# Windowed attention of a fused four-layer kernel: pairs of heads kept together, weights divided by the row sums, values on column halves

## The reference

```
p = softmax(concatenate([s_sink, s_meta, s_band]))      # s_sink: one learned number for each head
o = p[..., 1:1+16] @ meta_v + p[..., 17:] @ vband        # float32 throughout
```

## Time and profile before

| | us |
|---|---|
| median of 3 timed runs | 4331.46 (4327.49 to 4334.54) |
| the profiled execution | 4335.81 |
| its span, from the first to the last instruction | 4334.0 |
| PE busy | 4029.7 (93%) |
| DVE busy | 1845.5 (43%) |
| ACT busy | 1441.6 (33%) |
| mean granted clock of PE | 0.952 of full speed |
| sweep of layer 0, 2457.4 to 2625.8 | 168.4 |
| sweep of layer 1, 3561.4 to 3707.6 | 146.2 |

### The profile page before, as it was taken

The page is one execution under the profiler, slowest core; times in us unless marked ns, Lnnn a source line. Parts: engine busy times, 40 slices in busy tenths (PEclk is TensorE's granted clock), DMA queues, the critical chain, the costliest instruction groups (busy, mean ns, idle before and its releaser), DMA issues.

```text
span 4334.0 us, 66723 instructions
## 1 busy us (share of the span) xinstructions
PE 4029.7 (93%) x28114; PEld 3570.8 (82%) x28114; DVE 1845.5 (43%) x3401; ACT 1441.6 (33%) x2876; POOL 466.6 (11%) x529
## 2 busy tenths in 40 slices
PE   6988899999989999899989989979997998997998
PEld 6866678888878777788878869979996886997998
DVE  3443454323334444544445444343335544434344
ACT  3444443212233333332322343333232224434322
POOL 1211120000012222100010000020002000002001
PEclk8988899999989999999999979989998998998999
DMA  4022112222331110133311102322321110222332
GB/s 165 25 88 83 52 39 72 98 98 98 98 107 44 35 34 28 40 103 101 103 53 40 49 18 69 91 63 89 93 83 44 40 45 23 77 91 65 93 93 74
DMA packets 86762, 303.75 MB, mean 70 GB/s; under 512 B 9392, under 2 KB 12592, under 8 KB 86336
## 3 DMA queue, kind: packets, MB, share of 16 engines
q1 hardware_dynamic: 84944, 292.72, 21.5%
q0 software_dynamic: 1520, 6.75, 0.5%
HBM read 297.34 MB, written 2.10 MB: 69 GB/s over the span
## 4 chain that ended last, share of the span: by engine, by line
PE 87%; ACT 5%; DVE 3%; POOL 2%; issue 2%; DMA 2%; ACTq 0%; SPq 0%; DVEq 0%; POOLq 0%
PE bank L472 58%; PE bank L534 6%; PE bank L954 3%; PE bank L825 2%; PE bank L503 2%; PE bank L803 2%; PE bank L943 2%; PE bank L740 1%; POOL scratch L2402 1%; PE bank L779 1%; PE bank L1046 1%; PE bank L624 1%; PE bank L813 1%; PE bank L1019 1%; PE bank L685 1%
## 5 line engine op out<-in xcount | busy, mean ns | idle before, releaser
L1688 DVE TENSOR_TENSOR weight_lo<-weight_raw,weight_hi 128x1024 fp32r<-128x1024 f32 (+1 forms) x464 | 561.5, 1214 | 564.3 <-ACT weight_hi L1123 564.1
L472 PE MATMUL bank<-u_hi,weight_hi 128*128 128x256 f32 (+1 forms) x2368 | 692.3, 292 | 8.0 <-DVE u_lo L2342 5.8
L472 PE MATMUL bank<-u_lo,weight_hi 128*128 128x256 f32 (+1 forms) x2368 | 678.4, 286 | 0.0
L472 PE MATMUL bank<-u_hi,weight_lo 128*128 128x256 f32 (+1 forms) x2368 | 677.6, 286 | 0.0
L1123 ACT ACTIVATE weight_hi<-weight_raw 128x1024 fp32r<-128x1024 f32 (+1 forms) x464 | 476.3, 1031 | 504.9 <-PE bank L472 370.6
L472 PE MATMUL bank<-h_hi,weight_hi 128*128 128x512 f32 (+1 forms) x1360 | 500.1, 368 | 24.2 <-DVE h_lo L2073 12.9
L472 PE MATMUL bank<-h_lo,weight_hi 128*128 128x512 f32 (+1 forms) x1360 | 478.4, 352 | 0.0
L472 PE MATMUL bank<-h_hi,weight_lo 128*128 128x512 f32 (+1 forms) x1360 | 478.0, 351 | 0.0
L472 PEld LDWEIGHTS bank<-u_hi,weight_hi 128*128 128x128 f32 x2368 | 454.8, 192 | 27.4 <-issue 17.6
L472 PEld LDWEIGHTS bank<-u_hi,weight_lo 128*128 128x128 f32 x2368 | 454.8, 192 | 0.0
L472 PEld LDWEIGHTS bank<-u_lo,weight_hi 128*128 128x128 f32 x2368 | 453.7, 192 | 0.1
(11 more groups left out here) (270 smaller groups left out, 7587.3 us busy)
## 6 DMA issues: line engine op xcount, KB each, us to landing
weight_raw<-in_w_mlp SPq DMA_DIRECT2D x128, 512.0 KB, 3.6
weight_raw<-in_w_ff SPq DMA_DIRECT2D x128, 512.0 KB, 3.6
weight_raw<-in_w_in SPq DMA_DIRECT2D x92, 512.0 KB, 3.6
weight_raw<-in_w_mod SPq DMA_DIRECT2D x80, 512.0 KB, 3.9
weight_raw<-in_a_w_qkv SPq DMA_DIRECT2D x24, 512.0 KB, 4.3
weight_raw<-in_b_w_qkv SPq DMA_DIRECT2D x24, 512.0 KB, 3.6
first_weight<-in_w_mod SPq DMA_DIRECT2D x16, 512.0 KB, 14.7
weight_raw<-in_w_ret_o SPq DMA_DIRECT2D x16, 512.0 KB, 3.6
```

Of the source, the lines that this page charges most:

```text
L472: m = e.matmul(view[:, 0:hi - lo], a[:, k, :], b[:, k0 + k, lo:hi], start=(k == 0 and i == 0), stop=(k == kt - 1 and i == 2))
L1688: e.tensor_tensor(wlo[s][:, 0:kt, :], raw[n % N_RAW][:, 0:kt, :], whi[s][:, 0:kt, :].bitcast(F32), ALU.subtract).then_inc(*tick("dve_split ...
```

## The change

A unit is now a pair of heads: 20 units in layer 0 and 16 in layer 1, with three calls of `fill` for each as before, so that each call hands out twice as much. Scores are computed as before. DVE masks both heads and then takes both maxima. ACT takes both exponentials in place. DVE then takes one reciprocal of two sums and multiplies the weights of each head by theirs, in place, in SBUF. PE turns both heads' weights, ACT copies them to `WWT`, of which there is one buffer for each head (before, `PT` had two that alternated over the units). For the values the operands trade places: the 64 columns of `AV` of a head are stationary and its turned weights (128 queries) stream. Head 0 uses columns 0 to 63 of the array and head 1 columns 64 to 127, matmul by matmul in turn, into the two halves of one bank. The output comes out with features on the partitions, so that `AON`, the turn of the output (L1057) and the scaling of it (L2307) are gone; ACT copies the bank to `OA` at the beginning of the next unit.

```diff
-        AON = sb("win_rows", [P, 5, P], F32, o_z + 6 * HYB + 2560)
...
-        S_ = [W_S[:, 416 * i:416 * i + 416] for i in range(2)]
-        P_ = [W_S[:, 832 + 416 * i:832 + 416 * i + 416] for i in range(2)]
-        PT = [W_S[:, 1664 + 512 * i:1664 + 512 * i + 512] for i in range(2)]
-        QUERY_PAD = W_S[:, 2688:2944].rearrange("p (s c) -> p s c", s=2)
+        WS = [[W_S[:, 416 * (2 * i + s):416 * (2 * i + s) + 416] for s in range(2)] for i in range(2)]
+        WWT = [W_S[:, 1664 + 512 * s:1664 + 512 * s + 512] for s in range(2)]
...
-        WINDOW = [[(pr, qi, sub) for pr in range(4) for qi in range(5 - layer) for sub in range(2)]
-                  for layer in range(2)]
+        WINDOW = [[(pr, qi) for pr in range(4) for qi in range(5 - layer)] for layer in range(2)]
...
-                    pr, qi, sub = units[i]
-                    if sub:
-                        return
+                    pr, qi = units[i]
...
-                    views = [take("s", 2, layer, i + s) for s in range(2)]
...
-                                m.then_inc(*tick(("pe_scoreu", "pe_scorel")[s], ("s", 2, layer, i + s)))
-                    close("s", 2, layer, i)
-                    close("s", 2, layer, i + 1)
+                                m.then_inc(*tick(("pe_scoreu", "pe_scorel")[s], ("s", 2, layer, i, s)))
+                    for s in range(2):
+                        close("s", 2, layer, i, s)
...
-                    view = take("t", 2, layer, i)
-                    e.wait_ge(*at("w", 2, layer, i))
-                    Pr = P_[i % 2][0:nq]
-                    for j in range(len(ts)):
-                        e.transpose(view[:, P * j:P * j + nq], Pr[:, 17 + P * j:17 + P * j + P], ident[0:nq, 0:nq])
-                    e.transpose(view[0:N_META, 384:384 + nq], Pr[:, 1:17], ident[0:nq, 0:nq]).then_inc(
-                        *tick("pe_turn", ("t", 2, layer, i)))
-                    close("t", 2, layer, i)
+                    for s in range(2):
+                        view, x = take("t", 2, layer, i, s), WS[i % 2][s][0:nq]
+                        e.wait_ge(*at("n", 2, layer, i, s))
+                        for j in range(len(ts)):
+                            e.transpose(view[:, P * j:P * j + nq], x[:, 17 + P * j:17 + P * j + P], ident[0:nq, 0:nq])
+                        e.transpose(view[0:N_META, 384:384 + nq], x[:, 1:17], ident[0:nq, 0:nq]).then_inc(
+                            *tick("pe_turn", ("t", 2, layer, i, s)))
+                        close("t", 2, layer, i, s)
...
-                    pr, qi, sub = units[i]
...
-                    T_, gs = PT[i % 2], slice(HD * sub, HD * sub + HD)
...
+                    _, nq, ts, _ = geometry(units[i][1])
                     view = take("o", 2, layer, i)
-                    e.wait_ge(*at("wt", 2, layer, i))
+                    e.wait_ge(*at("wt", 2, layer, i, 0))
+                    e.wait_ge(*at("wt", 2, layer, i, 1))
                     e.wait_ge(*at("wvd", layer))
-                    e.matmul(view[0:nq, 0:HD], T_[0:N_META, 384:384 + nq], AV[0:N_META, 4, gs], start=True, stop=False)
-                    for n_, j in enumerate(ts):
-                        m = e.matmul(view[0:nq, 0:HD], T_[:, P * n_:P * n_ + nq], AV[:, j, gs],
-                                     start=False, stop=(n_ == len(ts) - 1))
+                    keys = [(4, N_META, 384)] + [(j, P, P * n) for n, j in enumerate(ts)]
+                    for k, (j, nk, c) in enumerate(keys):
+                        for s in range(2):
+                            r = slice(HD * s, HD * s + HD)
+                            m = e.matmul(view[r, 0:nq], AV[0:nk, j, r], WWT[s][0:nk, c:c + nq], start=(k == 0),
+                                         stop=(k == len(ts)))
                     m.then_inc(*tick("pe_value", ("o", 2, layer, i)))
                     close("o", 2, layer, i)
...
-                def turn_out(i):
-                    pr, qi, sub = units[i]
-                    _, nq, _, _ = geometry(qi)
-                    if sub == 1:
-                        view = take("ot", 2, layer, i)
-                        e.wait_ge(*at("out", 2, layer, i))
-                        e.transpose(view[:, 0:nq], AON[0:nq, qi, :], ident[0:nq, 0:nq]).then_inc(
-                            *tick("pe_value", ("ot", 2, layer, i)))
-                        close("ot", 2, layer, i)
-
-                sweep(len(units), (score, nothing, turn_weights, values, nothing, turn_out), fill)
+                sweep(len(units), (score, nothing, turn_weights, values, nothing, nothing), fill)
...
-                    n = 17 + P * len(ts)
-                    e.wait_ge(*at("max", 2, layer, i))
-                    if i >= 2:
-                        e.wait_ge(*at("t", 2, layer, i - 2))
-                    e.activation(P_[i % 2][0:nq, 0:n], S_[i % 2][0:nq, 0:n], ACT.Exp, bias=w_small(i, 0, nq),
-                                 accum_out=w_small(i, 1, nq)).then_inc(*tick("act_attn", ("w", 2, layer, i)))
+                    for s in range(2):
+                        x = WS[i % 2][s][0:nq, 0:17 + P * len(ts)]
+                        e.wait_ge(*at("max", 2, layer, i, s))
+                        e.activation(x, x, ACT.Exp, bias=w_small(i, s, nq), accum_out=w_small(i, 2 + s, nq)).then_inc(
+                            *tick("act_attn", ("w", 2, layer, i, s)))
...
-                    view, T_ = view_of("t", 2, layer, i), PT[i % 2]
...
-                    e.wait_ge(*at("t", 2, layer, i))
-                    if i >= 2:
-                        e.wait_ge(*at("o", 2, layer, i - 2))
-                    e.activation(T_[:, 0:P * len(ts)].rearrange("p (j c) -> p j c", c=P)[:, :, 0:nq],
-                                 view[:, 0:P * len(ts)].rearrange("p (j c) -> p j c", c=P)[:, :, 0:nq], ACT.Copy)
-                    e.activation(T_[0:N_META, 384:384 + nq], view[0:N_META, 384:384 + nq], ACT.Copy).then_inc(
-                        *tick("act_attn", ("wt", 2, layer, i), ("free", "t", 2, layer, i)))
+                    if i:
+                        e.wait_ge(*at("o", 2, layer, i - 1))
+                    for s in range(2):
+                        view, to = view_of("t", 2, layer, i, s), WWT[s]
+                        e.wait_ge(*at("t", 2, layer, i, s))
+                        e.activation(to[:, 0:P * len(ts)].rearrange("p (j c) -> p j c", c=P)[:, :, 0:nq],
+                                     view[:, 0:P * len(ts)].rearrange("p (j c) -> p j c", c=P)[:, :, 0:nq], ACT.Copy)
+                        e.activation(to[0:N_META, 384:384 + nq], view[0:N_META, 384:384 + nq], ACT.Copy).then_inc(
+                            *tick("act_attn", ("wt", 2, layer, i, s), ("free", "t", 2, layer, i, s)))
 
...
-                    if sub == 1:
-                        e.wait_ge(*at("ot", 2, layer, i))
-                        e.activation(OA[:, pr, q0:q0 + nq], view_of("ot", 2, layer, i)[:, 0:nq], ACT.Copy).then_inc(
-                            *tick("act_attn", ("free", "ot", 2, layer, i), ("oa", layer, pr)))
-
-                sweep(len(units), (score, expo, turn_weights, nothing, nothing, turn_out), fill)
+                    e.wait_ge(*at("o", 2, layer, i))
+                    e.activation(OA[:, pr, q0:q0 + nq], view_of("o", 2, layer, i)[:, 0:nq], ACT.Copy).then_inc(
+                        *tick("act_attn", ("free", "o", 2, layer, i)))
+
+                sweep(len(units), (score, expo, turn_weights, nothing, turn_out, nothing), fill)
...
-                    job = ("s", 2, layer, i)
-                    view, S = view_of(*job), S_[i % 2][0:nq]
-                    e.wait_ge(*at(*job))
-                    if i > 1:
-                        e.wait_ge(*at("w", 2, layer, i - 2))
-                        e.wait_ge(*at("out", 2, layer, i - 2))
-                    e.tensor_scalar(S[:, 1:1 + N_META], view[0:nq, 0:N_META], SCALE, None, ALU.mult)
-                    e.scalar_tensor_tensor(out=S[:, 17:17 + nb], in0=view[0:nq, N_META:N_META + nb], scalar=SCALE,
-                                           in1=mask, op0=ALU.mult, op1=ALU.add).then_inc(
-                        *tick("dve_attn", ("sc", 2, layer, i), ("free", *job)))
-                    e.wait_ge(*at("sc", 2, layer, i))
-                    e.wait_ge(*at("sink", layer, i))
-                    e.tensor_reduce(w_small(i, 0, nq), S[:, 0:17 + nb], AX, ALU.max, negate=True).then_inc(
-                        *tick("dve_attn", ("max", 2, layer, i)))
-
-                def values(i):
-                    pr, qi, sub = units[i]
-                    _, nq, ts, _ = geometry(qi)
-                    e.wait_ge(*at("w", 2, layer, i))
-                    e.reciprocal(w_small(i, 2, nq), w_small(i, 1, nq)).then_inc(*tick("dve_attn", ("rc", 2, layer, i)))
+                    for s in range(2):
+                        job = ("s", 2, layer, i, s)
+                        view, x = view_of(*job), WS[i % 2][s][0:nq]
+                        e.wait_ge(*at(*job))
+                        if i > 1:
```

(41 more changed lines are left out.)

10 lines of the change are left out of this document (5 added, 5 removed).

## The result

| | before | after |
|---|---|---|
| time, median (lowest to highest), us | 4333.0 (4327.49 to 4337.46), 4 runs | 4238.38 (4231.45 to 4239.26), 4 runs |
| ratio after / before, 95% interval | | 0.9779 (0.9762 to 0.9796) |
| both sweeps, us | 314.6 | 210.1 |
| PE busy / idle in them, us | 276.5 / 38.1 | 196.5 / 13.5 |

The account below looks back on a forecast made before the run. The prediction took the sweeps to be bound by PE, with stalls. Its terms, -48.7 - 7 + 2 + 4 = -49.7, rounded to -49, gave 4282 us, with a range of 4248 to 4316.

Parts of the forecast that it names:

- Work of PE: In both sweeps, 234.5 us at full clock, to fall by 41.3: 34.1 from values, 7.2 from the output's turn.
- Halves in turn: Rival for the values: column halves run in turn, not at once; 4312 to 4316 us, chance 0.03.
- With the share of half clock unchanged, 41.3 x 276.5 / 234.5 = 48.7 us.: Step for PE in the sweeps: saved full-clock work, stretched by an unchanged half-clock share, gives 48.7 us.
- the 0.80 to 0.92: Sign for both sweeps: a clock outside this range would show the prediction wrong; about 0.85 was expected.
- clock recovers: Rival for the sweeps: shorter stalls let the clock stay full, up to 34 us more saved; 4248 us, chance 0.11.
- I expect the long stalls to stay: Argument against the clock recovering in the sweeps; a long stall at 2578.5 to 2581 was followed by half clock.
- Taken together 0: Term for PE's stalls before the turns, 14.0 us in the kernel before: no net change, from -8 to +15.
- + 2 + 4: Terms in the total: scores, turns and fill up to +2; each layer's first unit waiting about 1.9 longer, +4.
- The places rotate, so 16 x 0.87 = 14 us: Term for stalls before the turns: 16 sigmoids with table loads, at rotating places in the fill, cost 14 us.
- A weight split that falls on a reload adds about 2: Term for stalls before the turns: a weight split of 1.04 us meeting a table reload adds about 2.
- The longer chain: Rival: the loop turn, copies, exponentials, multiply, next turn binds; 33 us come back, 4315 us, chance 0.14.
- 36 times 0.3 is 11 us: Term for PE's wait for ACT's copies before the values: 11 us against 17.9, so -7, bounds -18 and +5.

Follow-up runs that it names:

- e2: Kernel after with the two loops of the values swapped, so all key tiles of one column half precede the other's; 4260.76 us.
- e10: Kernel after with two added ACT copies of 384 columns in every unit, behind the wait for the second head's turned weights; 4263.75 us.
- e12: Kernel after with four added ACT copies of 960 columns in every fourth unit, behind the wait for the second head's turned weights; 4292.57 us.
- e6: Kernel before with a plain copy in place of the gates' sigmoid in the sweeps, those gates missing from the result; 4290.9 us.
- e3: Kernel before with heads in pairs and nothing else of the change: values as before, outputs divided instead of weights; 4291.75 us.
- e11: Kernel after with each weight tile multiplied once more, into a place that nobody reads; 4241.71 us.
- e4: Kernel before with each value matmul streaming all 128 columns of AV instead of 64, the others left unused; 4330.1 us.
- e9: e1 with each value matmul streaming all 128 columns of AV instead of 64, the others left unread; 4294.49 us.
- e1: Kernel after with the values computed as before and the turn of the output they need; weights still divided; 4294.33 us.

## Why the prediction was wrong

The direction and the mechanism of the values held; the size did not, by half.

**Work of PE: right, a little high.** PE was busy for 89.8 us of before's half clock, a share of 0.94 where the working took 0.88. Taken to full clock its work was thus 231.7 us and not 234.5, and it fell to 194.8, by 37 against 41.3 forecast. A pair with three band tiles takes 1.17 us from its start to the next instruction, against 1.08. Halves in turn were priced at 1.9 us for such a pair and 34.1 - 9 = 25 us more for the values. e2 has 2.28 from start to next and 33 us more of work, about what the values cost before the change; its time is only 22 more, since less is idle. The Trainium skill, TensorEngine Tiling (Array Packing), Key Properties, has the change of mode drain TensorE. The row above agrees with a small cost: 8 pairs of instructions at 0.118 are 0.95, and the rest of 1.17 is 0.22 for the step from 16 rows to 128 and the way back to full width together. No run separates the two, and what the entry costs does not show in it.

**The step that failed: "With the share of half clock unchanged, 41.3 x 276.5 / 234.5 = 48.7 us."** It took half clock as a tax on work, so less work paid less of it. The tax (half of PE's busy time at half clock) fell from 45 us to 2, 43 us less where the step allowed 7. The clock left the 0.80 to 0.92 that the prediction had set as a sign of being wrong. e10 and e12 show what it mostly hangs on here: long gaps of PE. At nearly the same idle sum the one has 13.7 us at half clock and the other 71.7. And e6 shows that in the kernel before the long gaps came from the table loads: none of them, no long gap, and 75 us less at half clock. The rival "clock recovers" had this mechanism and its 34 us, with a chance of 0.11. What spoke against it, "I expect the long stalls to stay", was the second error.

**"Taken together 0": the stalls before the turns.** They fell from 14.0 us to 6.3. (The sum carried + 2 + 4 for them, not the 0 of their own paragraph, and so expected 20.) The term that failed is "The places rotate, so 16 x 0.87 = 14 us". The working charged a sigmoid 1.1 us ahead of the copies, 1.5 between the copies and the exponentials, and nothing in the last fill. By ACT in order of time, 14 sigmoids stand in the two sweeps of after, and 9 of them in the last fill. Two stand ahead of the copies (2532.82 and 2555.64; the values then wait 0.92 and 0.40 us). Three stand between (2541.48, 2564.07, 3565.64), and PE waits 0.82, 2.23 and 0.64 for the multiply. At the working's own prices that is 2 x 1.1 + 3 x 1.5 = 6.7 us, not 14. In before, six stood between copies and exponentials, and they have 12.3 of the 14.0 us and all five long stalls. So the costly place is held by half as many, each at a smaller price; what part each has in it no run separates. A sigmoid in the last fill:

```profile
2524.23 0.19 ACT L1552 ACTIVATION_READ_ACCUMULATOR scratch<-scratch,small 128x1 f32 x1
2524.43 1.28 ACT L1469 ACT_TABLE_LOAD   x1
2525.73 0.40 ACT L1469 ACTIVATE hybrid_tmp<-bank 128x272 f32<-128x272 f32 x1
...
2527.53 0.49 ACT L1562 ACTIVATE scratch<-bank 128x384 f32<-128x384 f32 x1 [1.24 <-PE bank L1027]
...
2528.71 1.28 ACT L1552 ACT_TABLE_LOAD   x1
2530.01 0.63 ACT L1552 ACTIVATE scratch<-scratch,small 128x401 f32<-128x401 f32 x1
```

The load for the sigmoid starts straight behind the exponentials; load, sigmoid and one output copy are done by 2526.3, and ACT is then idle for 1.24 us before PE's turns release the copies. That part costs the chain nothing, as the working had it. The load back starts with the last copy's end and does lie on the chain, 1.28, but against a cover of two heads' values, fill and scores, 3.75 us by the prediction's own sum. The rows of before show the same order: a load at 2589.45, and 2.39 us of idle behind its sigmoid. The Trainium skill, ScalarE: Activation LUTs, What ACT_TABLE_LOAD costs, gives 2.66 us for a change of set, a load of 1.28 and a drain of 1.38. These rows show the load's 1.28 and no drain: the next ACTIVATE starts 1.30 after the load does.

ACT's idle time behind PE's turns, in layer 0, before and after (us, times, longest):

```profile
ACT scratch L1576 <- PE bank L1033: 86.0, 37, 5.9
```

```profile
ACT scratch L1562 <- PE bank L1027: 32.2, 17, 3.5
```

With one head at a time ACT had 86 us of idle and yet was late for PE: it could only work ahead by one head. The pair doubles what can be done at a time. e3, which has the pairs alone, shows the fall of PE's idle time from 38.1 to 18.5 us.

**The places where it was right about stalls.** "A weight split that falls on a reload adds about 2" is the longest stall of after. ACT, DVE and PE in order of time:

```profile
2562.78 1.28 ACT L1469 ACT_TABLE_LOAD   x1
...
2564.35 1.05 ACT L1109 ACTIVATE weight_hi<-weight_raw 128x1024 fp32r<-128x1024 f32 x1
2565.42 1.28 ACT L1552 ACT_TABLE_LOAD   x1
2566.72 0.52 ACT L1552 ACTIVATE scratch<-scratch,small 128x273 f32<-128x273 f32 x1
...
2568.14 0.63 DVE L2294 TENSOR_SCALAR scratch<-scratch,small 128x272 f32<-128x272 f32 x2
...
2568.65 0.66 PE L1026 MATMUL bank<-shape_constants,scratch 128*128 128x128 f32 x2 [2.23 <-DVE scratch L2294]
```

Load, sigmoid, split and load in a row, then the exponentials and the multiply; PE waits 2.23 us, and only here does after fall to half clock, for 3.4 us. The first units wait 1.7 (2468.20) and 0.7 us, where +1.9 each was forecast. The multiply of three band tiles took, in layer 0's sweep (busy us, mean ns, idle before):

```profile
L2294 DVE TENSOR_SCALAR scratch<-scratch,small 128x400 f32<-128x400 f32 x16 | 7.3, 498 | 0.3
```

The forecast had 0.40 for it, with bounds of 0.3 and 0.6. One takes 0.50 in the mean, or 0.46 of busy time. The longer chain, the rival at 0.14, did not come: e11 doubles the multiply for 3 us.

**"36 times 0.3 is 11 us": the stalls before the values.** They are 4.1 us in 13 waits over 0.15. Four of these, 0.92, 0.76, 0.40 and 0.26, are near sigmoids. In a plain unit with three band tiles PE waits 0.15 to 0.21 us where 0.35 was forecast, and with two 0.03 to 0.10 where it was 0.27: the four copies take 1.17 us (2527.53 to 2528.70) and not 1.30. Five units with a rotation or a second product in the fill do not wait at all, and neither do the meta tiles.

**The sum.** By the profiles, the sweeps lost 37 us of work (forecast 41), 43 of half clock (7) and 25 of idle (1). The clock and the idle time are largely one finding, since the long gaps are in both.

**Not settled.** Why e3 has 41.0 us at half clock and e10 13.7 with nearly as many long gaps (7 and 5, 13.1 and 9.4 us); part may be what single executions differ by, and a part may belong to the form of the values, by the 20 to 35 us that e4 and e9 show. No run separates the two. That the removed turn gave back clock by its long stalls is read from the traces of e1 and e3, and no run removes the turn alone. A long gap also does not always bring half clock: in after one of 1.71 us at 2468.20 did not.

## What to carry to other kernels

Where a window has a clock under 1, look for the long gaps of TensorE before pricing a change by its work: a change that splits or removes them can give back much of the half clock too, and one that makes them can cost about twice its idle time (e12, 54 us for 29 of added idle). Read where a table load starts, not only how long it is: it costs only what remains behind the engine's own idle time. And count at which place of the loop each one falls, in the order of the program, before taking a mean over the places. And where an engine is idle for long and is still waited for, put more work into each turn of the loop before making the work shorter: here pairing the heads alone gave 40 us.

## What the hardware showed that was not expected

- Doubling the streamed columns of an f32 product from 64 to 128, with 128 stationary, left the time of the kernel where it was: 4330.1 against 4333.0 us (e4), and 4294.49 against 4294.33 (e9). PE's work grew by 8 us and half clock shrank.
- A table load did not wait for the operand of the function that needs it. In after one started at 2550.83, straight behind the copies; the exponential behind it started at 2552.84, after 0.72 us of waiting for DVE's maximum.
- The two column halves overlap only in alternating order: 16 instructions in 1.24 us, or in 2.35 when one half's eight stand behind the other's.
